# Three moves in the page loop of a DeltaNet and MLA decode step: unit of the 16-bit split, order of the scores, halved reciprocal roots

## The reference, cut to what matters

```python
def mla_keys(latent, w_uk, w_uv, k_norm_nope):
    c = latent[..., :KV_LORA]; kr = latent[..., KV_LORA:]
    kn = rms_norm((c @ w_uk).reshape(bsz, s, MLA_HEADS, NOPE_DIM), k_norm_nope)
    ...
def page_block(phys):
    kn, kr, v = mla_keys(cache_l[phys], w_uk, w_uv, k_norm_nope)
    return partial_softmax(mla_scores(qn, qr, kn, kr), v)
```

## Time and profile before

| | |
|---|---|
| median of 3 runs | 1426.72 us (1419.31 to 1428.12) |
| profiled execution, its own time | 1426.71 us |
| its span | 1424.9 us |
| mean granted TensorE clock | 0.993 |
| PE busy | 1385.5 us (97%) |
| DVE busy | 1013.0 us (71%) |
| ACT busy | 859.0 us (60%) |
| POOL busy | 296.0 us (21%) |

### The profile page before, as it was taken

One profiled execution on the slowest core, in us unless ns is written; L12 is line 12 of the kernel. 1 busy time (PEld: TensorE's weight loads), 2 busy tenths in 40 slices (PEclk: granted clock), 3 DMA queues, 4 the chain that ended last, 5 costly groups with the idle time before them and its releaser, 6 DMA issues.

```text
span 1424.9 us, 30022 instructions
## 1 busy us (share of the span) xinstructions
PE 1385.5 (97%) x9428; PEld 1170.5 (82%) x9428; DVE 1013.0 (71%) x3674; ACT 859.0 (60%) x2780; POOL 296.0 (21%) x339
## 2 busy tenths in 40 slices
PE   8999999999999999999999999899999999999998
PEld 7877887877777777878778787678778999999998
DVE  5867667787877787777878777768666667777543
ACT  5536678686666866666865667566784453444332
POOL 3012222223332222322222312222241000000000
PEclk9999999999999999999999999999999999999999
DMA  9442326643457443365443463334644565555551
GB/s 284 119 118 57 92 53 146 161 104 73 95 116 162 105 98 76 87 154 125 93 108 85 107 141 83 74 80 104 178 89 157 167 237 177 178 178 177 177 180 59
DMA packets 282890, 180.05 MB, mean 126 GB/s; under 512 B 183072, under 2 KB 229696, under 8 KB 282728
## 3 DMA queue, kind: packets, MB, share of 16 engines
q1 hardware_dynamic: 282418, 177.86, 48.9%
q10 hardware_dynamic: 318, 0.33, 0.1%
HBM read 134.32 MB, written 6.77 MB: 99 GB/s over the span
## 4 chain that ended last, share of the span: by engine, by line
PE 78%; DVE 9%; ACT 8%; issue 3%; SPq 2%; DMA 1%; POOL 0%; DVEq 0%; ACTq 0%
PE ps L2058 13%; PE ps L2060 12%; PE ps L2059 12%; PE ps L2462 6%; PE ps L2463 6%; PE ps L2464 6%; ACT ksq L894 2%; PE ps L2133 2%; DVE prod L1284 2%; PE ps L2410 2%; PE ps L2411 2%; PE ps L2080 2%; PE ps L2134 2%; ACT cTr L881 2%; PE ps L2135 2%
## 5 line engine op out<-in xcount | busy, mean ns | idle before, releaser
L2058 PE MATMUL ps<-ukh,cTh 128*128 128x512 f32 x1024 | 418.7, 409 | 21.4 <-DVE sparts L1284 21.1
L894 ACT ACTIVATE ksq<-ps 128x128 f32<-128x128 f32 x1024 | 268.2, 277 | 243.3 <-PE ps L2060 242.9
L2060 PE MATMUL ps<-ukh,cTl 128*128 128x512 f32 x1024 | 402.2, 393 | 0.0
L2059 PE MATMUL ps<-ukl,cTh 128*128 128x512 f32 x1024 | 402.2, 393 | 0.0
L2058 PEld LDWEIGHTS ps<-ukh,cTh 128*128 128x128 f32 x1024 | 194.3, 190 | 77.7 <-issue 37.4
L1284 DVE CUSTOM_DVE_ANT_0 prod<-ps,qb 128x128 f32<-128x128 f32 x1024 | 234.9, 286 | 6.1 <-ACT ksq L894 5.1
L2060 PEld LDWEIGHTS ps<-ukh,cTl 128*128 128x128 f32 x1024 | 193.8, 189 | 43.0
L2059 PEld LDWEIGHTS ps<-ukl,cTh 128*128 128x128 f32 x1024 | 194.3, 190 | 34.2
L746 POOL TENSOR_TENSOR rk<-kss,mhalf 128x8 f32<-128x8 f32 x128 | 219.5, 1715 | 10.7
L894 ACT ACTIVATION_READ_ACCUMULATOR ksq<-ps 128x1 f32 x1024 | 212.9, 208 | 0.0
L881 ACT ACTIVATE cTr<-turned 128x1024 uint16<-128x1024 uint16 x126 | 174.6, 1386 | 3.6 <-DMA turned<-planes 3.6
(11 more groups left out here) (504 smaller groups left out, 2700.8 us busy)
## 6 DMA issues: line engine op xcount, KB each, us to landing
clat<-cache_mla SPq DMA_DIRECT2D x128, 256.0 KB, 2.6
wraw<-w_in SPq DMA_DIRECT2D x16, 1024.0 KB, 5.2
wraw<-w_up SPq DMA_DIRECT2D x16, 1024.0 KB, 5.4
wraw<-w_down SPq DMA_DIRECT2D x16, 1024.0 KB, 5.0
braw<-w_in SPq DMA_DIRECT2D x24, 512.0 KB, 4.1
crope<-cache_mla SPq DMA_DIRECT2D x128, 32.0 KB, 2.4
qb<-scratch SPq DMA_DIRECT2D x16, 256.0 KB, 3.7
sst<-state_gdn SPq DMA_DIRECT2D x32, 128.0 KB, 3.5
```

Source lines behind the costliest of these rows:

```text
L894: i = nc.scalar.activation(ksq[m % 3], ps[:, k % 3, P * h:P * h + P], ACT.Square, accum_out=kss[:, n // 4 % 2, n % 4, h0 + h:h0 + h + 1]). ...
L2058: mm(out, cTh[:, n % 2, c], ukh[:, c, cols], start=c == 0, stop=False)
L2059: mm(out, cTh[:, n % 2, c], ukl[:, c, cols], start=False, stop=False)
L2060: i = mm(out, cTl[:, n % 2, c], ukh[:, c, cols], start=False, stop=c == 3)
```

## The change

`split_planes` is written on ACT in place of DVE. It is the same copy with the same two waits, but it stands at the end of ACT's iteration, behind `squares(n,1)`, and no longer ahead of `scored(n,0)` on DVE. Page 2's copy stands behind ACT's `turned_page(0)`.

DVE's `scored(n-1,1)` (and the single `scored(0,0)`) now stands ahead of `split_lo(n+1)`.

`newton` is cut in two. `newton_start` waits for the root and does the reciprocal in steps 16 and 44; the rest (Newton step, high and low part) runs in the slot behind: the former empty slot behind step 16, now called ROOT, and step 45. A new semaphore `row_inverse` joins them. PE's waits for `row_rstd` stay in steps 17 and 46.

```diff
-STEPS = list(range(14)) + [None, 14, 15, 16, None] + list(range(17, 47))
+ROOT = 47
+STEPS = list(range(14)) + [None, 14, 15, 16, ROOT] + list(range(17, 47))
...
+            def split_planes(n):
+                act.wait_ge(S(f"page_landed{n % RING}"), 32 * (n // RING) + 32)
+                wait(act, "tr_landed", 16 * (n - 2))
+                nc.scalar.activation(planes[:].bitcast(U16).rearrange("p (x l) -> p x l", x=2), clat[:, n % RING, :].bitcast(U16).rearrange("p (l x) -> p x l", x=2), ACT.Copy).then_inc(S("planes_ready"), 1)
...
             turned_page(0)
+            split_planes(2)
             for n in range(NT):
...
                 beside(2 * n + 1)
                 squares(n, 1)
+                if n + 3 < NT:
+                    split_planes(n + 3)
...
-            def split_planes(n):
-                v.wait_ge(S(f"page_landed{n % RING}"), 32 * (n // RING) + 32)
-                wait(v, "tr_landed", 16 * (n - 2))
-                V.tensor_copy(planes[:].bitcast(U16)..., clat[:, n % RING, :].bitcast(U16)...).then_inc(S("planes_ready"), 1)
...
+            def newton_start(rows_, count):
+                v.wait_ge(S("row_sqrt"), count)
+                y = lr[0:rows_, 1]
+                V.reciprocal(y, y).then_inc(S("row_inverse"), 1)
+
             def newton(rows_, count, scale, sem):
-                v.wait_ge(S("row_sqrt"), count)
+                v.wait_ge(S("row_inverse"), count)
                 x, y, t_ = lr[0:rows_, 0], lr[0:rows_, 1], lt3[0:rows_]
-                link(V.reciprocal(y, y))
                 link(V.tensor_tensor(t_, y, y, ALU.mult))
...
                 if k == 16:
+                    newton_start(P, 2 * b + 1)
+                if k == ROOT:
                     newton(P, 2 * b + 1, consts[:, C_RSQ], "row_rstd")
...
                 if k == 44:
+                    newton_start(64, 2 * b + 2)
+                if k == 45:
                     newton(64, 2 * b + 2, 1.0, "row_rstd")
...
             split_lo(0)
-            split_planes(2)
             split_rope(0)
             for n in range(NT):
                 g, t = n // 4, n % 4
                 beside(2 * n)
-                if n + 1 < NT:
-                    split_lo(n + 1)
                 if n == 1:
                     scored(0, 0)
                 if n:
                     scored(n - 1, 1)
+                if n + 1 < NT:
+                    split_lo(n + 1)
...
                 beside(2 * n + 1)
-                if n + 3 < NT:
-                    split_planes(n + 3)
                 if n:
                     scored(n, 0)
```

More of the change, by code:

```diff
@@ L1255, in _ @@
             v.wait_ge(S("pool_clear"), 4)
-            def split_planes(n):
-                v.wait_ge(S(f"page_landed{n % RING}"), 32 * (n // RING) + 32)
-                wait(v, "tr_landed", 16 * (n - 2))
-                V.tensor_copy(planes[:].bitcast(U16).rearrange("p (x l) -> p x l", x=2), clat[:, n % RING, :].bitcast(U16).rearrange("p (l x) -> p x l", x=2)).then_inc(S("planes_ready"), 1)
             def split_rope(gg):
```

## The result

The changed kernel takes 1452.66 us (median of 4 runs, 1448.16 to 1457.22), the kernel before beside it 1427.03 (4 runs, 1419.31 to 1428.12): ratio 1.0189, 95% interval [1.0165, 1.0213]. That is 25.6 us slower, where 1430 was forecast and 1449 was the upper end. The profiled execution took 1448.16 us, the shortest of the four; its span of 1446.4 is 21.5 above the span of before, and 21.0 of these lie in the page loop. So what follows accounts for 21 us; the other 4 are the distance from this execution to the median.

What follows compares the result with a forecast made beforehand. PE, busy for 97% of the span, was taken to set the pace, with gains only where it waits for DVE. 1426.7 - 13.1 won + 16.0 lost = 1429.6, forecast 1430 us, own range 1418 to 1440, overall 1410 to 1449.

Steps and rivals of the forecast that it cites:

- The sum of what is lost: ACT's 1.39 us copy per page, paid in full stretches, last pages and pair ends: 16.0 us together.
- the delay of pairs 1 and 3: Activation stretches of pairs 1 and 3: full, but the already counted stall behind them absorbs the copy's delay; no loss.
- the early pages: Last pages before the pairs and the prompt's attention: the copy on ACT loses 2.5 us.
- the last: Last pages: little spare ACT time and the copy waiting for the page's landing lose 5 us.
- The steps for the roots: Divided roots in steps 44 and 16: shorter score waits, less the later rest, win 2.5 and 1.2 us.
- 619.02: PE's score wait there: the block moves off DVE, so 2.4 us and 1.7 of slow clock go, 4.1 won.
- the weights' low part: PE's waits for the low part of the pairs' weights: DVE is earlier, about half of 6.6 goes, 3 us.
- the tails: End of each pair, where pages have little other work: the copy's landing chain loses 0.5 us each, 2 in all.
- 806.74: PE's score wait at pair 2's step-44 root: it goes, since the score follows the reciprocal; 2.2 us.
- The term for the scores: Scores ahead of the low half: 1.8 us won at 111.96, nothing elsewhere.
- ACT has room enough: Faster rival: copies fit in ACT's 242.9 us of waiting for PE, waits go; 1399 to 1412 us, chance 0.22.
- The page's landing paces ACT: Slower rival: ACT's copy waits for a landing in one page of four; 1441 to 1460 us, chance 0.25.

Runs made afterwards that it cites:

- experiment 1: Kernel before with only the plane copy moved from DVE to ACT, orders and roots as before: 1451.95 us, ratio 1.0169.
- experiment 4: Changed kernel, but the rest of the step-16 root follows the score of its own slot, not the next: 1442.18 us, ratio 1.0108 to the kernel before.
- 8: Changed kernel with the root's rest behind the score of its own slot and all plane copies on DVE: 1417.67 us, ratio 0.9950 to the kernel before.
- experiment 3: Kernel before with only the divided roots, their rest in the later slot, planes on DVE: 1427.11 us, ratio 1.0007.
- experiment 9: Kernel before with DVE's plane copy cut to 8 of 512 columns from page 3 on: 1419.27 us, ratio 0.9956.
- experiment 6: Kernel before with only the copy's two waits (page landed, turn landed) added on ACT, no copy: 1425.69 us, ratio 1.0000.
- experiment 5: Kernel before with one more, unread copy on ACT that waits for no DMA, DVE keeping its own: 1465.24 us, ratio 1.0286.

## Why the prediction was wrong

Set against the table of stretches, its sum of +2.9 misses the loop's +21.0 by 18, in three places.

- **The step that failed most: the price of the copy on ACT.** The sum of what is lost put the delay of pairs 1 and 3 at nothing: "Pairs 1 and 3 are full too, but the stall behind them, which I have counted, takes the delay in." It does not. With the orders as before, the stall behind pair 1 grew from 2.63 to 3.53 us, and pages 47 to 51 became 4.1 us longer and 97 to 100 2.5 (experiment 1); with the scores first and the rest in its own slot the copy cost 1.3 and 2.4 there (experiment 4 against 8). The stall is itself a wait for scores whose squares and root ACT makes, so it comes later with ACT. In the net result these pairs grew by only 1.3 and 0.3, because the divided roots gave 1.7 and 1.6 back there (experiment 3). The other places were priced too low as well: pair 0 at 3 (4.1 in experiment 1), pair 2 at 3.5 (4.7), the early pages at 2.5 (5.2 in pages 0 to 16), the last at 5 (7.9). In all, the forecast netted the copy at +8: 16.0 lost less 7.6 for DVE's relief. It measured 24. Relief alone is worth 6 (experiment 9), so it is the 16.0 that was too small; an estimate from 24 + 6 is some 30, though the copy itself was shorter than priced.
- **The rest of the roots.** The steps for the roots won 3.7 us in the sum, with "about 1 us" and "0.9 each" for the later rest. In the trace it is 16.1 us of waits for `lrl`. The first root of pairs 0 and 2 (step 16) stands in no term of the sum, and there the longest came: 1.92 us ahead of 322.18 and 5.38 ahead of 711.79; with the roots alone they were 2.72 and 3.67 (experiment 3). What was not followed is what stands ahead of the rest in its new slot: the low half, behind `cTh`, behind the very copy that the same change puts on ACT. Alone the roots gave nothing (1.0007), with the copy they lost 9 us (1.0127 to 1.0189; the two intervals just meet) where 3.7 were to be won.
- **What was won was given back.** Pages 28 to 46, 52 to 71 and 77 to 96 were to bring 7.6 us by the roots, 619.02 and the weights' low part, less the tails. They cost 1.1. Page 66 with 619.02 did become 4.3 us shorter (4.1 said: right), and page 65 became 2.7 longer for the late root. In place of 806.74's wait of 2.24 and its dip came one of 2.78 for `rpT` and a longer dip. The low part of the weights won 1.0 of 3.

The term for the scores erred the other way: 1.8 us at one place were forecast, and alone the new order gave about 4.

**What was right.** The scores' waits (under 8; 6.5), the end of those near 421, 619 and 807, the first score (pages 0 and 1 together 1.8 us shorter; 1.8 said, though 1.27 us of a wait stays), and the last pages as a place, with ACT's copy waiting 4.62 us at 1022.62 and 3.46 at 1043.43. That their size fits too (+5.3; "5" less 0.5) is luck: the copy alone cost 7.9 there, and the other edits gave the rest back. New waits for the low half and `cTh` were to come to 10 to 20 us: the weight loads' for the low half reached 8.1, of which 4.0 stood before.

**The copy's duration.** 1.39 us was taken, the row of the same type with the step on the output, and 1.06 kept as the lower end; it is 1.07. The rule of the Trainium skill (ScalarE: Activation LUTs, What ACT_TABLE_LOAD costs) that gave 1.04 is borne out by this trace for a contiguous output read with a step, and not for `cTr`, which writes with one. By the forecast's own figure the error made the losses 4 us too large and hid part of the others.

**The rivals.** "ACT has room enough" read the mean: its 242.9 us of waiting for PE were real and 77 copies did fit in them for 4 us, but 48 did not. "The page's landing paces ACT" gave 1441 to 1460, and the time fell near it by another mechanism: ACT waited for landings 8 times and 22.3 us in all, not in each fourth page, and the waits alone cost nothing (experiment 6). The page cited with that rival (the Trainium skill, Perfetto Trace Analysis, Optimizing Scalar/DVE Operations: offload if DVE is saturated) points the right way here: relieving DVE, 71% busy, of 61 us gained 6, and moving the copy to ACT lost 23 or more in the net. By its own marks the forecast called itself wrong if the stretches of pairs 0 and 2 grew by other than 3 us each (3.7 and 5.4) and if the waits for `row_rstd` passed 2 us a pair (16.1 in four pairs).

## What to carry to other kernels

Before moving work to an engine with a lower mean, cut the loop into stretches of a few pages and compare length with that engine's busy time in each: where they are nearly equal, the added work can be paid nearly one for one (3.4 and 3.3 us for 3.7 in two stretches; over all of the 48 copies it was 20 us for 43); where they are not, it is nearly free (19 pages took 16.7 us more at the same length, 77 copies cost 4). Do not count a stall behind a full stretch as a cushion if the same engine feeds what is waited for: here it grew from 2.63 to 3.53 us. When one change moves two things, follow each moved instruction through its queue with the other edit made: the divided roots with their late rest cost nothing alone and 9 us behind the moved copy.

## What the runs showed of the hardware that was not expected

ACT's copy of 1024 16-bit elements takes 1074 ns with the step of two on its input and a contiguous output, and 1379 ns with the contiguous side read and the step on the output (both of the kernel after); DVE's took 685. The added copy of experiment 5, with its input stepped too, took 1075. The length of a wait alone does not tell whether the clock falls behind it. It fell to 0.51 behind the wait of 1.92 us ahead of 322.18, with another of 2.08 standing 2.5 us earlier (ahead of 319.64), and to 0.56 behind 5.38; it stayed at 1.00 behind the lone wait of 2.56 ahead of 624.21.
